# An encoder layer's MLP on one core: where the second token half's operands are formed, and the order of work on ScalarE and VectorE

## The reference

```python
    h = rms_norm(x, norm_mlp)
    x = x + jnp.square(jax.nn.relu(h @ w_ff1)) @ w_ff2     # w_ff1 1024x4096, w_ff2 4096x1024
```

## Time and profile before

| | us |
|---|---|
| median of 3 runs | 2460.48 |
| the profiled execution | 2461.04 |
| its span on the core | 2459.3 |
| TensorE busy | 2421.9 (98%) |
| VectorE busy | 1908.6 (78%) |
| GpSimd busy | 1379.1 (56%) |
| ScalarE busy | 1280.2 (52%) |
| mean granted TensorE clock | 0.997 |

### The profile page before, as it was taken

One profiled execution on the slowest core, in us unless ns is written; L12 is line 12 of the kernel. 1 busy time (PEld: TensorE's weight loads), 2 busy tenths in 40 slices (PEclk: granted clock), 3 DMA queues, 4 the chain that ended last, 5 costly groups with the idle time before them and its releaser, 6 DMA issues.

```text
span 2459.3 us, 38383 instructions
## 1 busy us (share of the span) xinstructions
PE 2421.9 (98%) x11936; PEld 2131.5 (87%) x11936; DVE 1908.6 (78%) x2664; ACT 1280.2 (52%) x2222; POOL 1379.1 (56%) x1106
## 2 busy tenths in 40 slices
PE   8999999999999999999999999999999899999999
PEld 6888888888777777778888889999999789999999
DVE  7986598888898787886676678777777977777777
ACT  7555112121677777773434446555556365555563
POOL 0004755563567666654444436666666576666665
PEclk9999999999999999999999999999999999999999
DMA  5445233222653122125656563222222252222222
GB/s 188 175 154 183 90 86 96 82 84 72 165 136 84 45 66 45 45 80 170 197 198 212 188 215 129 69 74 79 71 69 82 84 178 69 69 69 79 77 69 86
DMA packets 160262, 271.34 MB, mean 110 GB/s; under 512 B 47216, under 2 KB 63088, under 8 KB 159984
## 3 DMA queue, kind: packets, MB, share of 16 engines
q1 hardware_dynamic: 159824, 269.19, 35.5%
q10 hardware_dynamic: 288, 0.27, 0.0%
HBM read 200.08 MB, written 59.24 MB: 105 GB/s over the span
## 4 chain that ended last, share of the span: by engine, by line
PE 94%; DVE 3%; issue 1%; DMA 1%; POOL 1%; ACT 1%; SPq 0%; DVEq 0%; ACTq 0%; POOLq 0%
PE banks L63 9%; PE banks L64 9%; PE banks L65 9%; PE banks L3004 6%; PE banks L3007 6%; PE banks L3006 6%; PE banks L3028 6%; PE banks L3031 6%; PE banks L3030 6%; PE p_acc L63 4%; PE p_acc L64 4%; PE p_acc L65 4%; PE banks L1955 3%; PE banks L1954 3%; PE banks L1908 3%; PE banks L1923 3%
## 5 line engine op out<-in xcount | busy, mean ns | idle before, releaser
L2504 POOL TENSOR_TENSOR t_wlo<-f_s,t_whi 128x512 fp32r<-128x512 f32 x256 | 360.8, 1412 | 186.5 <-ACT t_whi L2535 186.2
L1743 POOL TENSOR_TENSOR a_plo<-a_p,a_phi 128x512 fp32r<-128x512 f32 x236 | 306.0, 1306 | 147.7 <-DVE a_phi L1874 144.0
L2768 DVE TENSOR_TENSOR f_x<-banks,f_x 128x384 f32<-128x384 f32 x448 | 240.7, 551 | 111.5 <-PE banks L3031 111.5
L2495 POOL TENSOR_TENSOR t_wlo<-t_wraw,t_whi 128x1024 fp32r<-128x1024 f32 x67 | 164.1, 2450 | 218.9 <-ACT t_whi L2520 218.9
L3004 PE MATMUL banks<-block,t_whi 128*128 128x384 f32 x720 | 243.3, 338 | 5.4 <-DVE banks L2913 2.5
L2535 ACT ACTIVATE t_whi<-f_s 128x512 fp32r<-128x512 f32 x256 | 161.2, 631 | 162.6 <-PE banks L3031 133.3
L1789 ACT ACTIVATE a_p<-banks 128x512 f32<-128x512 f32 x320 | 190.6, 596 | 101.2 <-PE banks L1955 93.7
L3007 PE MATMUL banks<-block,t_wlo 128*128 128x384 f32 x720 | 241.6, 335 | 0.0
L3006 PE MATMUL banks<-block,t_whi 128*128 128x384 f32 x704 | 236.3, 336 | 0.0
L3028 PE MATMUL banks<-block,t_whi 128*128 128x384 f32 x608 | 206.4, 340 | 14.9 <-DVE f_x L2768 9.3
L3031 PE MATMUL banks<-block,t_wlo 128*128 128x384 f32 x608 | 205.3, 338 | 0.0
(11 more groups left out here) (375 smaller groups left out, 7157.7 us busy)
## 6 DMA issues: line engine op xcount, KB each, us to landing
t_wraw<-w_tail_t SPq DMA_DIRECT2D x136, 512.0 KB, 3.9
a_quotient<-w_tail_t SPq DMA_DIRECT2D x64, 512.0 KB, 4.0
block<-roped_scratch SPq DMA_DIRECT2D x146, 128.0 KB, 2.7
w_raw<-w_in_t SPq DMA_DIRECT2D x31, 512.0 KB, 3.9
proj_scratch<-s_gate SPq DMA_DIRECT2D x48, 256.0 KB, 2.1
t_graw<-proj_scratch SPq DMA_DIRECT2D x24, 512.0 KB, 3.8
p_sw<-p_qn SPq DMA_DIRECT2D x60, 128.0 KB, 2.1
roped_scratch<-p_r_hi SPq DMA_DIRECT2D x30, 256.0 KB, 2.2
```

Of the source, the lines that this page charges most:

```text
L1743: pool.tensor_tensor(p_lo[s][:], p32[s][:], f32(p_hi[s][:]), ALU.subtract).then_inc(plo_pool, 1)
L2504: pool.tensor_tensor(weights_of(t, ring_lo[t % 4]), source(t), f32(weights_of(t, ring_hi[t % 4])), ALU.subtract).then_inc(lo_pool.sem, 1)
L2768: dve.tensor_tensor(to, ps[:, f2_bank(sb_of(it), it.d, j), 0:QN], to, ALU.add).then_inc(f2_added, 1)
```

## The change

There is a new DRAM scratch `quart_d` of 4 x 7 x 128 x 384 float32 for the 28 operands of the second half. They are formed in twelve strips (four kt by three strips of 128 tokens), at the loops `strip_at` = 21; 39, 49; 67, 77; 95, 105; 123, 133; 151, 161; 179 of the first half: SP loads a strip with two DMAs four loops earlier, VectorE scales it with two instructions in loop `at` (`scale_strip`) and forms four sums of 128 columns in loop at + 1 (`strip_sums`), and SP stores it with two DMAs in loop at + 3. The right part of `stage[0]` holds the strip. From loop 192 on SP loads the 28 operands back, one a loop, each into the place of its low; ScalarE makes one high a loop from 196 on (`later_high`), VectorE the lows of even number (14) one loop behind, in every second loop (`later_low`), POOL the 14 of odd number in loops 200 to 226.

On ScalarE `f_high(t + 3)` moves to the front of the loop, ahead of the snaps and squares, for all t. T4's lows of the first half move from VectorE's loops 1 and 2 to 3 and 4. For slow pairs the sums T1 and T3 move from 16 and 17 loops after the pair's start to 9 and 10, the sum T4 from 20 to 22, its high from 21 to 23, its low from 22 to 24.

The diff, cut to its core (`quarter_sums` and `mix_high` lose their branches for the second half):

```diff
 PREP = (B11, B22, B21, T1, T2, T3, T4)
-LATER = (B21, B11, B22, T3, T4, T1, T2)
-ON_POOL = (T1, T2)
+QUARTERS = (B11, T3, B21, B22, T1, T2, T4)
+LENT = ((0, 2), (0, 3), (1, 2), (1, 3), (2, 2), (2, 3), (3, 3))
+LATER = [(d, kt) for d in range(7) for kt in range(KH) if (d, kt) not in LENT] + list(LENT)
+STRIP = QN // 3
 SPLIT = (B11, B22, T1, T3, B21, T2, T4)
...
         self.prep_at = self.sb_at[0, 2 * FF_GROUPS - 4]
-        self.late_lows = {self.prep_at + 7 * kt + 7 + i: (kt, c) for kt in range(KH) for i, c in enumerate(ON_POOL)}
+        self.late_lows = {self.prep_at + i + 3: i for i in range(1, len(LATER), 2)}
+        strips = [self.sb_at[0, 0]]
+        for g in range(1, FF_GROUPS - 2):
+            strips += [self.sb_at[0, 2 * g] - 10, self.sb_at[0, 2 * g]]
+        self.strip_at = strips + [self.start[FF_PAIRS - 3] + 4]
         self.f1_before, self.f2_before, self.pool_before = [0], [0], [0]
...
+        strip, strip_t4 = st.stage[0][:, 2 * QN:].rearrange("p (r c) -> p r c", c=STRIP), fsb("f_t4", [P, STRIP])
         rs2 = st.stage[1][:, 0:BLK]
...
+        def later_low_done(eng, d):
+            i = max(LATER.index((d, kt)) for kt in range(KH))
+            mixed_lo.wait(eng, 28 + i // 2 + 1)
+            lo_pool.wait(eng, feed.late_low_count(i if i % 2 else i - 1))
...
+        HIGH_AT = ((7, 7, 9, 9, 10, 11, 12), (15, 15, 17, 18, 19, 20, 23))
...
-            def load_stage(h, kt):
-                view = stage_at(h, kt)[:].rearrange("p (k n) -> p k n", k=2)
-                rows = lambda t, n0, n1: t[kt:kt + KH + 1:KH, :, n0:n1].rearrange("k p n -> p k n")
-                if h == 0:
-                    if kt:
-                        st_in.wait(sp, 16 * kt)
...
+            def load_strip(i):
+                kt, j = divmod(i, 3)
+                if i == 0:
+                    mixed.wait(sp, 4 * KH)
+                    mixed_lo.wait(sp, 7 * KH)
+                x1_out.wait(sp, 16 * 4 * NBLK + 32 * i)
+                for n, of in enumerate((normed_d if j < 2 else x1_d, x1_d)):
+                    at = HALF + n * QN + j * STRIP
+                    sp.dma_start(strip[:, n:4:2], of[kt:kt + KH + 1:KH, :, at:at + STRIP].rearrange("k p n -> p k n")
+                                 ).then_inc(st_in.sem, 16)
+            def store_strip(i):
+                kt, j = divmod(i, 3)
+                mixed.wait(sp, 4 * KH + 4 * (i + 1))
+                at = slice(j * STRIP, (j + 1) * STRIP)
+                sp.dma_start(quart_d[kt, 0:6, :, at].rearrange("c p n -> p c n"), strip).then_inc(x1_out.sem, 16)
+                sp.dma_start(quart_d[kt, 6, :, at], strip_t4[:]).then_inc(x1_out.sem, 16)
+            def load_later(i):
+                d, kt = LATER[i]
+                if i == 0:
+                    x1_out.wait(sp, 16 * 4 * NBLK + 32 * 3 * KH)
+                if i >= 4:
+                    later_in[i % 4].wait(sp, 16 * (i // 4))
+                if (d, kt) in LENT:
+                    sp.wait_ge(f2_done, lent_free[d, kt])
                 else:
-                    sp.dma_start(view[:, :, 0:2 * BLK - HALF], rows(normed_d, HALF, 2 * BLK)).then_inc(st_in.sem, 16)
-                    sp.dma_start(view[:, :, 2 * BLK - HALF:], rows(x1_d, 2 * BLK, TOK)).then_inc(st_in.sem, 16)
...
-                at = t - feed.prep_at
-                if at == -1:
-                    sp.wait_ge(alo_ready, 7 * (FF_PAIRS - 1))
-                    load_stage(1, 0)
-                elif at in (6, 13, 20):
-                    stage_free(1, at // 7)
-                    load_stage(1, at // 7 + 1)
+                for i, at in enumerate(feed.strip_at):
+                    if t == at - 4:
+                        load_strip(i)
+                    elif t == at + 3:
+                        store_strip(i)
+                if 0 <= t - (feed.prep_at - 4) < len(LATER):
+                    load_later(t - (feed.prep_at - 4))
             sp.wait_ge(y_out, 16 * 4 * KD)
...
-                    kt, c = feed.late_lows[t]
-                    mixed_hi.wait(pool, mixed_count(1, kt, LATER.index(c)))
-                    pool.tensor_tensor(place[1][c, kt, 1], part(1, kt, c), f32(place[1][c, kt, 0]),
-                                       ALU.subtract).then_inc(lo_pool.sem, 1)
+                    i = feed.late_lows[t]
+                    hi, lo = (place[1][*LATER[i], k] for k in range(2))
+                    mixed_hi.wait(pool, 28 + i + 1)
+                    pool.tensor_tensor(lo, f32(lo), f32(hi), ALU.subtract).then_inc(lo_pool.sem, 1)
...
+            def later_high(i):
+                hi, lo = (place[1][*LATER[i], k] for k in range(2))
+                later_in[i % 4].wait(act, 16 * (i // 4 + 1))
+                act.activation(hi, f32(lo), ACT.Copy).then_inc(mixed_hi.sem, 1)
...
-                    mixed_lo.wait(act, low_count(1, KH - 1, 4))
                 act.activation(aside(pg) if k == 0 else z, z, ACT.Square).then_inc(r_done.sem, 1)
             for t in range(3):
                 f_high(t)
             for t in range(END + 2):
+                if t + 3 < END:
+                    f_high(t + 3)
...
                         squared(pg, min(d - 5, 3))
-                if t + 3 < END:
...
-                at = t - feed.prep_at
-                if 0 <= at < 7 * KH:
-                    kt, step = divmod(at, 7)
-                    if at == 3:
-                        f1_done.wait(act, 7 * FF_PAIRS)
-                    elif at == 17:
-                        act.wait_ge(f2_done, 2 * 7 * (2 * FF_GROUPS - 2))
-                    for c in {3: LATER[0:3], 4: LATER[3:5], 5: LATER[5:7]}.get(step, ()):
-                        mix_high(1, kt, c)
+                if 0 <= t - feed.prep_at < len(LATER):
+                    later_high(t - feed.prep_at)
                 if t < 2:
...
+            def four_sums(b11, b12, b21, b22, t1, t2, t3, t4, n):
...
+            def scale_strip(i):
+                kt, j = divmod(i, 3)
+                st_in.wait(dve, 16 * KH + 32 * (i + 1))
+                dve.wait_ge(rs_ready, NBLK)
+                for side in range(2):
+                    k = kt + KH * side
+                    if j < 2:
+                        new, by = strip[:, 2 * side + 1], rs2[:, (j + 1) * STRIP:(j + 2) * STRIP]
+                    else:
+                        new = strip[:, 2 * side:2 * side + 2]
+                        by = rs2.rearrange("p (r c) -> p r c", c=STRIP)[:, 0::3]
+                    dve.scalar_tensor_tensor(new, new, gn[:, k:k + 1], by, ALU.mult, ALU.mult).then_inc(hn_ready.sem, 1)
+            def strip_sums(i):
+                hn_ready.wait(dve, 2 * KD + 2 * (i + 1))
+                four_sums(*(strip[:, r] for r in (0, 1, 2, 3, 4, 5, 1)), strip_t4[:], 4 * KH + 4 * i)
+            def later_low(i):
+                hi, lo = (place[1][*LATER[i], k] for k in range(2))
+                mixed_hi.wait(dve, 28 + i + 1)
+                dve.tensor_tensor(lo, f32(lo), f32(hi), ALU.subtract).then_inc(mixed_lo.sem, 1)
...
-                         {16: ((B11, 1), (T1, 0)), 17: ((B22, 1), (T3, 0)), 18: ((T1, 1),), 19: ((T3, 1), (T2, 0)),
-                          20: ((B21, 1), (T4, 0)), 21: ((T2, 1),), 22: ((T4, 1),)})[feed.slow(pg)]
+                         {9: ((T1, 0),), 10: ((T3, 0),), 16: ((B11, 1),), 17: ((B22, 1),), 18: ((T1, 1),),
+                          19: ((T3, 1), (T2, 0)), 20: ((B21, 1),), 21: ((T2, 1),), 22: ((T4, 0),),
+                          24: ((T4, 1),)})[feed.slow(pg)]
                 for d, low in steps.get(back, ()):
...
-                if i == 0:
-                    st_in.wait(dve, 16 * KH + 32 * (kt + 1))
-                    dve.wait_ge(rs_ready, NBLK)
-                new = stage_at(1, kt)[:].rearrange("p (k n) -> p k n", k=2)[:, i, 2 * BLK - HALF:]
-                k = kt + KH * i
-                dve.scalar_tensor_tensor(new, new, gn[:, k:k + 1], rs2, ALU.mult, ALU.mult).then_inc(hn_ready.sem, 1)
-            def prepare(at, late_half):
-                if not 0 <= at < 7 * KH:
-                    return
-                kt, step = divmod(at, 7)
-                if step == 1:
-                    scale_new(kt, late_half)
-                elif step == 2:
-                    for _ in range(2 - late_half):
-                        next(sums_of[kt], None)
-                elif step == 4:
-                    if late_half:
-                        next(sums_of[kt], None)
-                    quarter_low(1, kt, LATER[late_half])
-                elif step == 5:
-                    quarter_low(1, kt, LATER[2 + late_half])
-                elif step == 6 and late_half:
-                    quarter_low(1, kt, LATER[4])
...
-                for pg, back in feed.pairs_near(t, 8, 22):
+                for pg, back in feed.pairs_near(t, 8, 24):
                     finish(pg, back)
-                if t in (1, 2):
-                    for kt in (2 * t - 2, 2 * t - 1):
-                        quarter_low(0, kt, T4)
+                if t in (3, 4):
```

(47 more changed lines are left out.)

108 lines of the change are left out of this document (40 added, 68 removed).

## The result

The changed kernel takes 2447.34 us, the median of 7 runs (2445.84 to 2454.55), the kernel before in the same comparison 2460.82 (7 runs, 2459.17 to 2466.51). The ratio is 0.9949, interval 0.9937 to 0.9961: 0.5% faster, where 2434.0, 1.1%, was forecast, and outside the range of 2427 to 2445. The profiled execution took 2447.34 us, its span is 2445.6.

A forecast was written before the change was run, and what follows sets the result against it. TensorE held 94% of the wait chain, with VectorE the bound in items 196 to 224; 2461.04 - 21 (forming) - 7 (seams) + 1.5 (strips) + 0 + 0 = 2434.5, less 0.56 gives a 2434.0 us median, range 2427 to 2445.

The forecast's parts named there:

- the strips' term: VectorE's six instructions for each of twelve strips, taken to cost +1.5 us in all, bounds 0 to +8.
- The forming stage: Items 196 to 224, from 86.7 to 65.3 us as forming leaves them: -21 us, bounds -14 to -26.
- under 3 was the sign given: Sign that the forecast is right: TensorE's wait for evictions (L2768 before) in items 196 to 224 under 3 us.
- the trace's rule: Each VectorE instruction with two SBUF inputs costs POOL 0.38 us, about half its length; POOL's 52.2 us grow to 64.
- The seams: Two short pauses, 0.26 and 0.32 us, ending each of twelve groups should go: -7 us, bounds 0 to -7.
- The first pair: MLP's first pair, with ScalarE's and VectorE's new orders: 0 us, bounds -2.5 to +2.5.
- that pause comes out of the later one: First pair: a new wait of some 1.8 us at item 2 is taken off the later pause, net 0.
- ScalarE's order elsewhere: Snap for item 4 of pairs after a fast one, behind a high: 0 us, bounds 0 to +3.6.
- ScalarE's order becomes a wait: Rival: item 2 waits, a half-clock stretch follows, later pause stays, 18 snaps cost 0.2 each: +7, 2441 us; chance 0.10.
- Slower: the strips stop TensorE: Rival: strip instructions queue behind POOL at groups' first evictions, 46 us lost in place of 1.5: 2478 us; chance 0.03.
- Full exclusion of VectorE and POOL: Rival: in the forming stage the two never overlap; it ends near 72 us, kernel 2441 us; chance 0.22.

The follow-up runs named there:

- the three together: Changed kernel with the six group-start strips five items later, the weights' high behind snaps and squares, T4's first-half lows in loops 1 and 2: median 2432.09 us.
- the forming alone: Changed kernel with the high, T4's lows and the slow pairs' steps and highs as in the kernel before, keeping forming in strips: 2446.03 us profiled.
- strips moved: Changed kernel with the six strips of the group starts moved five items on: 2433.15 us profiled, items 21 to 195 in 364.8 us.
- changed again: The changed kernel, same program, profiled a second time: 2453.06 us profiled, median of 8 runs 2452.14 us.
- both with moved strips: Two variants of the changed kernel, the six group-start strips five items later (2433.15 us profiled) or one loop earlier (2432.91 us).
- T1 and T3 late: Changed kernel with the slow pairs' sums T1 and T3 back at 16 and 17 loops after the pair's start: 2446.64 us profiled.
- T4's lows early: Changed kernel with T4's lows of the first half back in VectorE's loops 1 and 2: 2451.33 us profiled.
- orders alone: Kernel before with the weights' high first on ScalarE, T4's lows in loops 3 and 4, and the slow pairs' new steps: 2453.20 us profiled.
- both balances: Two variants of the changed kernel splitting the 28 operand lows 7 on VectorE, 21 on POOL (2444.20 us profiled) or 21 and 7 (2449.02 us).

## Why the prediction was wrong

**The step that failed is the strips' term.** It was taken as +1.5 us with bounds 0 to +8, on the ground that VectorE has idle time and that an eviction may be 2 us late; at the group starts it measured +14.0 (378.8 against 364.8). Two things in it were wrong. The strip's own VectorE time was inside the estimate: the twelve take 12.9 + 10.2 + 6.4 + 6.2 + 3.5 + 3.4 = 42.6 us in the rows below (four sums, two kinds of scaling), 3.55 us a strip between the 1.4 and 5.8 given.

```profile
L2727 DVE TENSOR_TENSOR stage<-stage 128x128 f32<-128x128 f32 x12 | 12.9, 1078 | 0.0
L2760 DVE SCALAR_TENSOR_TENSOR stage<-stage,t_gain 128x128 f32<-128x128 f32 x16 | 10.2, 675 | 0.0
L2731 DVE TENSOR_TENSOR stage<-stage 128x128 f32<-128x128 f32 x12 | 6.4, 536 | 0.4
L2760 DVE SCALAR_TENSOR_TENSOR stage<-stage,t_gain 128x256 f32<-128x256 f32 x8 | 6.2, 813 | 0.0
L2729 DVE TENSOR_TENSOR stage<-stage 128x128 f32<-128x128 f32 x12 | 3.5, 292 | 0.4
L2732 DVE TENSOR_TENSOR f_t<-stage 128x128 f32<-128x128 f32 x12 | 3.4, 283 | 0.0
```

What was set against it, 99.7 us of VectorE's idle time over 175 items, was the wrong measure: the question is what else stands in the same two or three loops. The weight sums come in loops 1 to 4 of each seven, so in loops 22 to 25 in group 0, and the change itself moved T1 and T3 "early in the group", into loops 23 and 24. For the stage 196 to 224 it had made just that count, loop by loop, and was right. Second, it took the meeting with POOL as an added price for the strip alone. The strip also made the weight sums late, and these then met POOL as well.

**Rightly forecast.** The forming stage: 66.2 us against 65.3, TensorE's wait for evictions

```profile
PE banks L3048 <- DVE f_x L2809: 3.9, 7, 0.9
```

in place of 9.3 us (under 3 was the sign given), VectorE 97% busy, POOL 90%, no half-clock stretch. By the trace's rule POOL's 52.2 us were to grow to 64; they grew to 59.5. The seams: both pauses of the earlier trace rows are gone in all twelve groups. Where neither a strip nor ScalarE's order costs time (the three together) the two halves are 2.8 us (367.5 to 364.7) and 3.2 us (468.0 to 464.8) shorter, 6.0 of the 7.0.

**The first pair** was 0 with bounds of 2.5; items 0 to 20 measured +3.0. The 1.8 us ahead of item 2 came as worked out (1.77 idle in the weight load). That "that pause comes out of the later one" held for item 6 only in part (1.24 in place of 1.84 us), and the pause ahead of item 13, of pair 1, which had no term, grew by 1.9. Of T4's lows the prediction said that the same instructions stand ahead "in another order"; that order alone makes 2.5 us of pauses. With the old place of both, items 0 to 20 take 49.7 again (the three together, the forming alone).

**ScalarE's order elsewhere** was "just in time", 0 to 0.2 for 18 pairs. It is 0.2 to 0.6 us at the last pair of each half, 0.6 at pair 1 (pauses of 0.2 and 0.4 us ahead of items 9 and 11), and nothing at the other pairs.

**The rivals.** "ScalarE's order becomes a wait" was true as a mechanism, with 3.0 and at most 1.2 us in place of 7. "Slower: the strips stop TensorE" named the right place and was true to a third: it set the point at 2.4 us a strip for all twelve; measured were 2.3 us (14.0/6) at the six group starts and nothing at the other six. It should have had a case of its own between the two: the strips pause TensorE, and half the gain is lost. Full exclusion of VectorE and POOL in the forming stage gave 72 us; measured were 66.2, and with 21 lows on POOL 65.6. By that rival's sum the latter would be 38.0 + 21 x 1.015 of POOL and 7 x 0.55 + 16 x 0.68 + 1.1 of VectorE, 75 us. So the two engines do overlap: what the meeting costs is less than the sum of the durations. The Trainium skill ("SBUF — State Buffer", section "Who interferes with whom") adds that issue order decides who blocks. The timelines agree, 0.68 us for the weight sum that starts ahead of POOL (strips moved) and 1.64 for the one that starts behind it (the changed kernel).

Beside all this, 4.7 us of the profiles' difference of 13.7 lie ahead of the MLP, in code that is the same, and say nothing of the change. What it does by the profiles is 9.0 to 10.6 us in the MLP: with the start of the kernel before, the changed kernel's profile would have taken some 2452 us, farther from the forecast.

**What stays open.** The half-clock stretch after item 13's pause comes in some profiles (items 0 to 20 at 52.8 us: changed, changed again, both with moved strips) and not in others whose pauses up to there are the same (51.2 to 51.3: T1 and T3 late, T4's lows early, orders alone, both balances). No run tells what decides it. Why the pause ahead of item 13 grows with either order was not traced either.

## What to carry to other kernels

Before putting work "where the engine is idle", list what else that engine does in the same two or three loops, and what in its queue TensorE waits for: moving six strips by one loop was worth 13.6 us, and two parts that gain 12.1 and 3.4 us alone gain 9.0 together, 5.5 us of the difference in the stage where both moved work into the same loops. Where VectorE and GpSimd both read SBUF, look at who starts first: in the timelines a few tenths late cost VectorE's instruction 0.6 to 1.0 us, and a few tenths early cost GpSimd's 0.3; no run here changes that order alone. A queue order changed for all loops (a high ahead of the snaps) needs a stage in which it gains: here it gained in none.
